# Gated layers: the per-head normalisation placed behind the next decode state sum; pooling layer: old rows copied ahead of the norm

## What is computed

```python
def gla_mixer(h, s0, w_in, w_a2, b_a, g_on, w_out):      # layers 0 and 3
    q, k, v, g, a = _split(h @ w_in, ...)
    logf = log_sigmoid(a @ w_a2 + b_a) / 16
    o, s = gla_recurrence(q * GDK**-0.5, k, v, logf, s0)  # chunks of 64 tokens
    o = rmsnorm(o, g_on)          # per token and head, 256 values each
    return (o * silu(g)) @ w_out, s

def pool_mixer(h, prefix, ...):                           # layer 2
    u, g = _split(h @ w_in, [1024, 1024])
    ext = concat([prefix, u])     # prefix: the last 15 rows before the segment
    d = trailing means of ext over 2, 4, 8, 16 rows, minus u
    return ((d @ w_grp) * scale * silu(g)) @ w_out, ext[-15:]
```

## Time and profile before

| | before |
|---|---|
| median of 3 runs | 1239.66 us |
| the profiled execution: its own time | 1239.08 us |
| its span | 1237.3 us |
| mean granted clock of PE | 0.978 |
| PE / PEld busy | 1178.9 us (95%) / 1038.0 us (84%) |
| DVE / ACT / POOL busy | 595.8 (48%) / 568.3 (46%) / 381.1 us (31%) |
| moved by transfers | 168.78 MB, mean 136 GB/s |

### The profile page before, as it was taken

How to read it: one execution, slowest core, us unless ns; L and a number is a source line. 1 busy time by engine, 2 the same in 40 slices (tenths; PEclk the granted TensorE clock), 3 DMA queues, 4 the chain that set the end, 5 groups by cost and what they waited for, 6 DMA issues and landing times. The chain is left out here.

```text
span 1237.3 us, 25049 instructions
## 1 busy us (share of the span) xinstructions
PE 1178.9 (95%) x9935; PEld 1038.0 (84%) x9935; DVE 595.8 (48%) x1179; ACT 568.3 (46%) x1100; POOL 381.1 (31%) x322
## 2 busy tenths in 40 slices
PE   6999999999999999999979999999999999999897
PEld 5789887897768998889974458999999889987796
DVE  4362344756049999200014553569355353245642
ACT  6442367643233355444553453422444244266753
POOL 5445131145123421122200004444434353411330
PEclk8999999998899999999998999999999999999998
DMA  5334235133313356676668974323222135234211
GB/s 149 103 103 154 86 103 171 59 78 96 114 65 122 107 178 210 213 238 207 221 238 332 357 271 134 100 69 103 87 82 65 35 103 188 69 110 147 86 35 73
DMA packets 132909, 168.78 MB, mean 136 GB/s; under 512 B 25545, under 2 KB 98601, under 8 KB 132784
## 3 DMA queue, kind: packets, MB, share of 16 engines
q1 hardware_dynamic: 120729, 152.59, 37.9%
q10 hardware_dynamic: 12062, 14.59, 3.4%
HBM read 150.70 MB, written 16.81 MB: 135 GB/s over the span
## 5 line engine op out<-in xcount | busy, mean ns | idle before, releaser
L664 POOL TENSOR_TENSOR w_lo<-raw,w_hi 128x512 fp32r<-128x512 f32 (+2 forms) x267 | 359.2, 1376 | 759.8 <-ACT w_hi L1367 759.8
L700 PE MATMUL psum<-h_hi,w_hi 128*128 128x272 f32 x1616 | 472.0, 292 | 9.5 <-DVE h_lo L2206 4.6
L702 PE MATMUL psum<-h_hi,w_lo 128*128 128x272 f32 x1616 | 468.0, 290 | 0.0
L701 PE MATMUL psum<-h_lo,w_hi 128*128 128x272 f32 x1616 | 465.4, 288 | 0.0
L700 PEld LDWEIGHTS psum<-h_hi,w_hi 128*128 128x128 f32 x1616 | 304.0, 188 | 20.7 <-issue 12.5
L701 PEld LDWEIGHTS psum<-h_lo,w_hi 128*128 128x128 f32 x1616 | 304.5, 188 | 0.0
L702 PEld LDWEIGHTS psum<-h_hi,w_lo 128*128 128x128 f32 x1616 | 303.6, 188 | 0.0
L1367 ACT ACTIVATE w_hi<-raw 128x1024 fp32r<-128x1024 f32 (+1 forms) x137 | 135.2, 1034 | 121.7 <-PE psum L702 86.6
L700 PE MATMUL psum<-w_hi,h_hi 128*128 128x512 f32 (+2 forms) x352 | 125.8, 357 | 0.0
L701 PE MATMUL psum<-w_lo,h_hi 128*128 128x512 f32 (+2 forms) x352 | 122.4, 348 | 0.0
L702 PE MATMUL psum<-w_hi,h_lo 128*128 128x512 f32 (+2 forms) x352 | 122.3, 347 | 0.0
(11 more groups left out here) (309 smaller groups left out, 1487.1 us busy)
## 6 DMA issues: line engine op xcount, KB each, us to landing
raw<-in_cache_k_dram SPq DMA_DIRECT2D x128, 256.0 KB, 3.2
raw<-in_gla_w_in_dram SPq DMA_DIRECT2D x23, 1024.0 KB, 5.5
spare<-in_cache_v_dram SPq DMA_DIRECT2D x36, 512.0 KB, 5.5
raw<-in_dsa_w_in_dram SPq DMA_DIRECT2D x17, 1024.0 KB, 6.2
raw<-in_cache_v_dram SPq DMA_DIRECT2D x28, 512.0 KB, 5.0
gla_s_in<-in_state_gla_dram SPq DMA_DIRECT2D x16, 512.0 KB, 7.9
raw<-in_gla_w_out_dram SPq DMA_DIRECT2D x8, 1024.0 KB, 6.9
out_dram<-gla_s_in ACTq DMA_DIRECT2D x16, 512.0 KB, 4.2
```

Source lines behind the costliest of these rows:

```text
L664: pool.tensor_tensor(copies(key, pair_view(w_lo, key)[:, k]), raw_copies(key, k), copies(key, pair_view(w_hi, key)[:, k].bitcast(F32)), AL ...
L700: pe.matmul(out, lh, rh, start=start, stop=False)
L701: pe.matmul(out, lh, rl, start=False, stop=False)
L702: return pe.matmul(out, ll, rh, start=False, stop=stop)
```

## The change

Three edits.

1. In the gated layers DVE's `root(t)` and `normalise(t)` leave the end of the pass t and go into the next pass: for t = 0 and 1 behind `sequence(2t+2)` and `gate_part(4t+6)` of that pass, ahead of its `add_state`; for t = 2 to the head of the last pass, ahead of `sequence(6)`, which is where they were.
2. ACT's stream gets a `preload_act_table_set(EXP_LN)` ahead of each of the three roots per gated layer, six in all.
3. In the pooling layer ACT's `norm(L)` goes behind the two waits and the eight copies of the old rows.

```diff
@@ scalar, gla @@
                         gate_block(2 * t + 1)
                         sequence(2 * t + 1)
+                        act.preload_act_table_set(EXP_LN)
                         root(slice(4 * t, 4 * t + 4), t)
                         gate_block(2 * t + 2)
@@ scalar, pooling @@
             def pooling(L):
-                norm(L)
-
                 act.wait_ge(*on("stores_v", "all"))
                 act.wait_ge(*on("stores_ik", "all"))
                 for half in range(2):
...
                             .then_inc(*sig("u_old", L, half))
+                norm(L)
@@ vector, gla @@
                 for t in range(NP_T):
+                    if t == NP_T - 1:
+                        root(slice(4 * t - 4, 4 * t), t - 1)
+                        normalise(t - 1)
                     sequence(2 * t)
                     gate_part(4 * t + 2)
+                    if 0 < t < NP_T - 1:
+                        root(slice(4 * t - 4, 4 * t), t - 1)
+                        normalise(t - 1)
                     if t < NP_T - 1:
                         add_state(2 * t + 2)
...
                     sequence(2 * t + 1)
                     gate_part(4 * t + 5)
-                    root(slice(4 * t, 4 * t + 4), t)
-                    normalise(t)
                 sequence(DB - 1)
```

## The result

The changed kernel takes **1227.82 us** (median of 4 runs, 1226.16 to 1228.76) against 1239.74 us for the kernel before on the same chip; the ratio is 0.9903, interval 0.9883 to 0.9923. The forecast was 1232.1, the range began at 1228: the kernel is faster, as forecast, but by 11.9 us and not by 7.5, and the time lies 0.2 us outside the range. The three edits did what the prediction says, 7.6 us against 7.3; what its sum left out is TensorE's clock.

The account below looks back on a forecast made before the run. PE, busy 95% of the span, was taken to bound the kernel. Attention stalls of 4.84 us plus pooling's 2.49 gave 7.3 us off 1239.08, or 1231.8 (1232.4 from the median); forecast 1232.1, range 1228 to 1237.

Parts of the forecast that it names:

- Four stalls of L984: Gated layers' attention stages: PE's four waits for DVE's decode state sum go, 4.84 us off.
- The pooling's 2.49: Pooling layer's start: PE's idle at L700 for ACT's copies of the old rows goes, 2.49 us off.
- The wait of 1.25 us stays as it is: PE's wait for decode state 7 before L1018 moves with PE's work; change taken as 0.
- Price the added queueing at 0: DVE's moved root and normalise fit ahead of add_state with 0.8 us of room; cost 0, at most 3.2 us.
- The sum of 7.3: Whole kernel: 4.84 us from attention stalls plus 2.49 us from pooling, taken off 1239.08 us.
- Of this nothing is on PE's path: Gated layers' roots: six fewer ACT table loads save 7.7 us of ACT but are priced 0 for PE.
- Gain lost in layer 1: Rival: DVE's and ACT's steps in layer 1 absorb the first layer's 2.4 us; about 1234.5 us, chance 0.08.
- State 7's load taking the place: Rival: PE's wait before L1018 grows 2.4 us in both layers, leaving only the pooling gain; 1236.6 us, chance 0.08.
- The rival of a shorter half rate stretch on top: Less half-rate time for PE: up to 4 us more gain, 1228 us and a little under; chance 0.08.
- the clock's term of the sum: PE's granted clock: no amount in the forecast sum, though shifting layer 1's half rate stretch was said to change its length.
- at most 8 us: Layer 1, 300 to 316 us: 16 us at half rate worth at most 8 us of PE work.
- the opposite turn: Rival: a longer half rate stretch in layer 1 cancels the gain or more, 1240 to 1243 us; chance 0.10.

Follow-up runs that it names:

- a3: Only the pooling layer's old-row copies moved ahead of the norm, on the kernel before; ratio 0.9956.
- b1: Only the three table preloads per gated layer added to the kernel before, root and normalise left in place; ratio 0.9946.
- e: The changed kernel run again, unchanged, for more executions and a second trace; ratio 0.9923 against the kernel before.
- a1: Root move and table preloads in layer 0 only, on the kernel before; ratio 0.9943.
- b2: Only root and normalise moved in both gated layers, without preloads or the pooling change, against the kernel before; ratio 0.9965.
- c2: The changed kernel with layer 1's index matmuls spread between the k projection's tiles; ratio 1.0006 against the kernel before.
- a2: Root move and table preloads in layer 3 only, on the kernel before; ratio 0.9981.
- a4: The kernel before run once more, unchanged, for a second trace; ratio 0.9986.
- d: The changed kernel with 20 transposes of layer 0's output repeated; ratio 0.9914 against the kernel before.
- c1: The changed kernel with decode state 7 loaded ahead of the last output weight; ratio 0.9934 against the kernel before.
- h2: The changed kernel with three of layer 1's sums-of-squares matmuls added again, 1.4 us of work; ratio 0.994 against the kernel before.
- h1: The kernel before with three of layer 1's sums-of-squares matmuls added again, 1.4 us of work; ratio 0.9976.
- g1: The kernel before with ten of layer 1's sums-of-squares matmuls added again, 4.6 us of work; ratio 1.001.
- g2: The changed kernel with six of layer 1's sums-of-squares matmuls added again, 2.8 us of work; ratio 0.9955 against the kernel before.

## Why the prediction was right and wrong

**The places right, to a tenth.** Four stalls of L984, 4.84 us: 4.9 by the traces, 5.3 at equal clock (after less a3). The pooling's 2.49: 2.7 by the trace and 2.3 ±0.7 by a3 alone. "The wait of 1.25 us stays as it is": 1.25. "Price the added queueing at 0", with 0.8 us of room: 0.85 of idle left ahead of L2095. The sum of 7.3 came out as 7.6.

**The table edit right with edit 1, and incomplete without.** "Of this nothing is on PE's path" holds only because edit 1 had taken DVE's wait away first. On the kernel before, b1, the tables alone are worth what edit 1 is worth. The prediction costed each edit on top of the other and did not say that they are the same gain twice.

**The rivals.** Gain lost in layer 1: it did not come. State 7's load taking the place: not in after, but in layer 0 PE waits 1.05 us for it in e's trace and 0.56 in b1's, where after, a1 and b2 have no such wait. The rival of a shorter half rate stretch on top came, and it is the result.

**The step that failed** is the clock's term of the sum. The sum adds the stalls and the pooling and nothing for the granted clock; the clock stands only among the rivals, at "up to 4 us more" with a chance of 0.08. Measured, it is 3.5 us in the mean of 11 executions against 123 and 3.0 us in the profiled pair, where the index stage gives 5.7 and other stretches take 2.8 back. The stretch of the earlier trace rows is 17.1 us long and worth 7.3 us when it is wholly absent: from the first L1086 to L807 it is 27.48 us before and 20.22 in a1 (316.23 - 296.01). So "at most 8 us" was a fair bound, and halving it to 4 had no row behind it. A chance of 0.10 for the opposite turn and 0.08 for this one treated the two alike, although the stretch was there already, and none of the 16 traces shows it longer than 17.1 us.

A part of the miss is the start of the sum. The mean of 11 executions, 1226.8, is 5.3 us under the forecast: 3.5 are the clock, 0.3 the edits, and 1.4 are that the forecast set out from 1239.4 (between 1239.08 and 1239.66), where 123 executions of before have a mean of 1238.0. With the clock's part and the range's end at 1228, no room was left for the other two; that the time lies 0.2 us outside and not inside is chance.

**What it misread.** The prediction has matmuls in the earlier trace rows "that wait for DVE and ACT results before them", and calls the stage "the least dense of the kernel". Neither is in the rows: PE waits 0.7 us in the stage in after and not at all in before. c2 was built on that reading and missed.

The Trainium skill's "TensorE: Matmul & The Clock Gate", Part 1, says that the gate's timing is not tied to the kernel's start and that the slow matmuls vary from run to run. That is borne out in part: 123 executions of the kernel before spread over 1229.5 to 1246.4 us, with clocks of 0.974 to 0.988, and the stretch begins at 299.1 us in one trace of it and at 297.6 in the other. But the index stage is not hit at random. In all four traces in which layer 0 is unchanged and nothing is added (before, a2, a3, a4) the stretch is there, 17.1 us long; in six of the seven with layer 0 changed and nothing added in layer 1 (a1, b1, b2, after, e, d) it is absent or 3.4 us long, and in the seventh, c1, it is there with its 17.1 us.

| start of the index stage, us | half rate stretch in it, us |
|---|---|
| before 296.97, a4 296.24, a2 296.06, a3 299.37 | 299.1 to 316.1, 297.6 to 314.6, 298.1 to 315.2, 300.5 to 317.6 |
| a1 296.01, b1 296.55, b2 293.59, e 294.65 | none |
| after 295.87, d 296.06 | 305.2 to 308.6, 305.4 to 308.8 |
| c1 294.23, h2 296.34 | 295.2 to 312.3, 298.1 to 315.1 |
| h1 300.20, g1 304.05, g2 298.98 | none |

**What stays open.** The start of the stage, counted from the kernel's start, does not decide: a2 at 296.06 has the stretch, a1 at 296.01 has not. That agrees with the rule that the gate's timing is not tied to the kernel's start. The traces also differ in half rate stretches in their first 62 us, and I could not tell whether these set what comes 240 us later or only move the stage. That 1.4 us of added work is enough to turn the mean clock either way is shown by h1 and h2; why just the shift of the change falls on the good side is not. One trace stands for each kernel, while its clock varies between executions. Mean clocks over all executions agree with the traces by groups, with two exceptions: a3's is 0.9813, above before, with the stretch in its trace, and g2's is 0.9803 without it.

## What to carry to other kernels

When an in-order engine makes TensorE wait, look for the ready instruction behind the unready one: moving the unready one back by one ready step, or shortening what it waits for, was worth the whole stall here, and once one is done the other was worth nothing here. A stage that already runs at half rate is a term of the sum with two signs, here as large as the edits that shift it: price it at all that the stretch can give back, and compare variants at equal mean clock, or a shift will pass for a gain. Before an experiment adds a delay, look in the trace for a wait in front of it that will swallow it.

## What the runs showed of the hardware

- The same 1.4 us of extra work ahead of the index stage changed the mean time by -3.0 ±2.3 us in one kernel (h1) and by +5.0 ±2.7 us in the other (h2).
- Where a half rate stretch began 1.0 to 2.1 us behind that stage's first matmul, it lasted 17.1 us, in all six traces (before, a2, a3, a4, c1, h2), and the 24 matmuls took 750 to 804 ns each instead of 491. Where it began 9.3 us behind (after, d), it lasted 3.4 us. DVE and ACT did the same work in the same time in the windows of a1 and a2.
- PE was busy in all of that slow stage in before, and waited 0.7 us of it in after: busy time alone did not tell a stage at half rate from one at full rate.
- Three runs are not enough to name the kernel before: their median of 1239.66 lies 1.6 us above the mean of 123 executions, whose standard deviation is 3.6 us.
- A repeated full precision matmul of 272 columns (two records in the trace) took 0.46 us when repeated (g1, 4.6 us for ten); 0.23 had been planned.
